# Rotary embedding of the retention heads in three pieces instead of one, with a second buffer

## The reference

```
h = rmsnorm(x, g_mix[l])
proj = h @ w_in[l]                      # split in q_r, k_r, v_r, g_r, q_s, k_s, v_s, gate_a, gate_b
q_r = rotary(q_r by 4 heads of 128)     # t1, t2 = the two halves of a head
k_r = rotary(k_r by 4 heads of 128)     # [t1*cos - t2*sin, t1*sin + t2*cos]
ret = retention(q_r, k_r, v_r)          # scores = q_r k_r * decay, times v_r
sb  = stick_breaking(q_s, k_s, v_s)     # weights from exp(log_beta + reversed cumulated sum)
merged = sigmoid(gate_a) * (norm(ret) * silu(g_r)) @ p_ret + sigmoid(gate_b) * sb @ p_sb
x = x + merged @ w_out ; x = x + relu(rmsnorm(x) @ w_up)^2 @ w_down
```

## Time and profile before

| | |
|---|---|
| median of three runs | 1245.2 us (1245.06 to 1245.97) |
| the profiled execution, its time | 1246.07 us |
| its span, first to last instruction | 1244.3 us |
| granted TensorE clock, mean | 0.998 |
| PE busy | 1213.6 us, 98% of the span |
| PEld busy | 1062.6 us, 85% |
| DVE busy | 890.3 us, 72% |
| ACT busy | 631.0 us, 51% |
| POOL busy | 56.3 us, 5% |
| DMA queue of the weights | 219.04 MB, 54.6% of 16 engines |

### The profile page before, as it was taken

One profiled execution on the slowest core, in us unless ns is written; L12 is line 12 of the kernel. 1 busy time (PEld: TensorE's weight loads), 2 busy tenths in 40 slices (PEclk: granted clock), 3 DMA queues, 4 the chain that ended last, 5 costly groups with the idle time before them and its releaser, 6 DMA issues.

```text
span 1244.3 us, 17057 instructions
## 1 busy us (share of the span) xinstructions
PE 1213.6 (98%) x6810; PEld 1062.6 (85%) x6810; DVE 890.3 (72%) x1040; ACT 631.0 (51%) x823; POOL 56.3 (5%) x70
## 2 busy tenths in 40 slices
PE   5999999999999999999999999999989999999998
PEld 4888888888888887888888888888879998988886
DVE  5577798888666676777888777666677766766665
ACT  4454576635343344555677445434458457443442
POOL 1000120001000000000220001000010000100000
PEclk9999999999999999999999999999999999999999
DMA  6854545555655656655555555565646334655552
GB/s 233 272 158 147 169 147 159 179 192 171 201 186 186 202 169 216 193 146 163 164 150 164 200 172 194 178 200 189 200 167 195 102 102 136 202 181 192 202 181 107
DMA packets 163082, 219.85 MB, mean 177 GB/s; under 512 B 5712, under 2 KB 134224, under 8 KB 163024
## 3 DMA queue, kind: packets, MB, share of 16 engines
q1 hardware_dynamic: 163024, 219.04, 54.6%
HBM read 217.98 MB, written 1.05 MB: 176 GB/s over the span
## 4 chain that ended last, share of the span: by engine, by line
PE 70%; issue 18%; DVE 5%; ACT 4%; DMA 2%; POOL 1%; SPq 0%; POOLq 0%; DVEq 0%; ACTq 0%
PE ps L497 69%; DVE w_lo L1317 2%; ACT w_hi L888 1%; DMA raw<-in_w_in_dram 1%; DMA decay_c<-in_decay_dram 1%; PE ps L532 1%; POOL retqkv L1284 1%; ACT junk L902 0%; DMA gain<-in_g_mix_dram 0%; DVE xs L1363 0%; DVE retqkv L1494 0%; DVE hT L1323 0%; ACT hz L1086 0%; ACT htmp L1094 0%; DVE htok L1347 0%
## 5 line engine op out<-in xcount | busy, mean ns | idle before, releaser
L1317 DVE TENSOR_TENSOR w_lo<-raw,w_hi 128x1024 fp32r<-128x1024 f32 x402 | 486.3, 1253 | 93.3 <-ACT w_hi L888 93.2
L888 ACT ACTIVATE w_hi<-raw 128x1024 fp32r<-128x1024 f32 x402 | 402.3, 1052 | 187.0 <-DMA raw<-in_w_up_dram 120.6
L497 PE MATMUL ps<-hT,w_hi 128*128 128x512 f32 (+1 forms) x1952 | 426.3, 365 | 6.8 <-DVE gr L1329 3.5
L497 PEld LDWEIGHTS ps<-hT,w_hi 128*128 128x128 f32 x1952 | 339.7, 190 | 62.2 <-issue 4.7
L497 PE MATMUL ps<-w_hi,uT 128*128 128x512 f32 x768 | 244.0, 390 | 0.0
L497 PE MATMUL ps<-hT,w_lo 128*128 128x256 f32 x1696 | 239.8, 283 | 0.0
L497 PEld LDWEIGHTS ps<-hT,w_lo 128*128 128x128 f32 x1696 | 225.4, 192 | 7.0
L894 ACT ACTIVATE carry<-ps 128x512 f32<-128x512 f32 x114 | 67.9, 596 | 261.8 <-PE ps L497 261.7
L497 PEld LDWEIGHTS ps<-w_hi,uT 128*128 128x128 f32 x768 | 144.4, 188 | 29.7 <-DVE uT L1323 0.6
L497 PE MATMUL ps<-w_lo,uT 128*128 128x512 f32 x384 | 149.9, 390 | 0.0
L497 PE MATMUL ps<-w_hi,hT 128*128 128x512 f32 (+1 forms) x480 | 142.3, 374 | 5.9 <-DVE w_lo L1317 4.5
(11 more groups left out here) (194 smaller groups left out, 920.2 us busy)
## 6 DMA issues: line engine op xcount, KB each, us to landing
raw<-in_w_in_dram SPq DMA_DIRECT2D x77, 1024.0 KB, 5.7
raw<-in_w_up_dram SPq DMA_DIRECT2D x48, 1024.0 KB, 5.3
raw<-in_w_down_dram SPq DMA_DIRECT2D x48, 1024.0 KB, 4.9
raw<-in_w_out_dram SPq DMA_DIRECT2D x12, 1024.0 KB, 4.9
raw<-in_p_sb_dram SPq DMA_DIRECT2D x8, 1024.0 KB, 5.2
raw<-in_p_ret_dram SPq DMA_DIRECT2D x8, 1024.0 KB, 5.0
xs<-in_x_dram SPq DMA_DIRECT2D x2, 512.0 KB, 6.4
gain<-in_g_mix_dram SPq DMA_DIRECT2D x2, 512.0 KB, 6.9
```

What stands on the lines that cost most here:

```text
L497: return pe.matmul(o, lhsT, rhs, start=start, stop=stop)
L888: act.activation(w_hi[:, s, half], raw[:, s, half], ACT.Copy).then_inc(hi_ready, 1)
L1317: last = dve.tensor_tensor(w_lo[:, s, half], raw[:, s, half], w_hi[:, s, half].bitcast(F32), ALU.subtract)
```

## The change

`rotate` becomes three steps with places of their own in `stages`: `swap` (ACT's exchange of the halves and POOL's cosines), `sines` (DVE's product with the sines) and `rotate` (DVE's sum). For the queries they stand at k = 16, 17 and 18, for the keys at k = 18, 19 and 20. On ACT `swap` is moved out of the stage function and is done before the conversion of piece k + 3. The keys' exchange writes into `gates[:, 0, 0:4, :]`, which lies idle then, instead of `ry`, and ACT's waits for `rest_split` and `rope_done` are gone.

```diff
-            if k in (18, 19):
-                todo.append(("rotate", k - 18))
+            for i in range(2):
+                for name, at_piece in (("swap", 16), ("sines", 17), ("rotate", 18)):
+                    if k == at_piece + 2 * i:
+                        todo.append((name, i))
...
+        def swapped(i):
+
+            return gates[:, 0, 0:4, :] if i else ry[:, :, :, :].rearrange("p a e t -> p (a e) t")
...
-                    elif name == "rotate":
-
-                        act.wait_ge(pair_free, use_of("rk", 1, L).count(3))
-                        act.wait_ge(rest_split, Place(3, (L, SB_H // 2)).count(1))
-                        if i:
-                            act.wait_ge(rope_done, Place(0, (L, 2)).count(1))
-                        swapped = ry[:, :, :, :].rearrange("p a e t -> p (a e) t")
-                        act.activation(swapped[0:P // 2], retqkv[P // 2:P, :, i, :], ACT.Copy)
-                        act.activation(swapped[P // 2:P], retqkv[0:P // 2, :, i, :], ACT.Copy).then_inc(turned, 1)
...
+                    for name, j in stages(k):
+                        if name == "swap":
+
+                            act.wait_ge(pair_free, use_of(("rq", "rk")[j], 1, L).count(3))
+                            act.activation(swapped(j)[0:P // 2], retqkv[P // 2:P, :, j, :], ACT.Copy)
+                            act.activation(swapped(j)[P // 2:P], retqkv[0:P // 2, :, j, :], ACT.Copy).then_inc(turned, 1)
                     if k < MIX_PIECES - 1:
                         convert(piece + AHEAD)
...
-                        elif name == "rotate":
+                        elif name == "swap":
 
                             pool.wait_ge(turned, Place(i, (L, 2)).count(1))
...
-                    elif name == "rotate":
-                        part = Place(i, (L, 2))
+                    elif name == "sines":
+                        part, tmp = Place(i, (L, 2)), swapped(i)
                         dve.wait_ge(turned, part.count(1))
                         dve.wait_ge(consts_in, 32)
-                        v, tmp = retqkv[:, :, i, :], ry[:, :, :, :].rearrange("p a e t -> p (a e) t")
                         dve.tensor_tensor(tmp, tmp, rope_c[:, 1:2, :].to_broadcast([P, RET_H, T]), ALU.mult).then_inc(rope_sin, 1)
+                    elif name == "rotate":
+                        part, v = Place(i, (L, 2)), retqkv[:, :, i, :]
                         dve.wait_ge(rope_cos, part.count(1))
                         dve.wait_ge(rope_sin, part.count(1))
-                        dve.tensor_tensor(v, v, tmp, ALU.add).then_inc(rope_done, 1)
+                        dve.tensor_tensor(v, v, swapped(i), ALU.add).then_inc(rope_done, 1)
```

## The result

| | before | after |
|---|---|---|
| median, runs beside each other | 1245.59 us (1245.06 to 1246.09) | 1260.16 us (1258.05 to 1260.96) |
| ratio after to before, 95% interval | | 1.0102 [1.009, 1.0114] |
| span of the profiled execution | 1244.3 us | 1258.6 us |
| granted TensorE clock, mean | 0.998 | 0.992 |

The change makes the kernel slower, as forecast, but by 14.6 us where 10.0 were forecast, and 1260.2 lies above the range, which ended at 1257.5.

What follows compares the result with a forecast made beforehand. PE, busy 98%, was taken to bound the kernel. Per layer -2.1 + 2.1 + 1.3 + 2.3 + 1.4 = +5.0 us, +10.0 in two layers, on 1245.2 gives 1255.2 us; range 1247.5 to 1257.5.

Steps and rivals of the forecast that it cites:

- What bounds: PE, busy 98% of the span; its late waits for `gr` at pieces 21 and 22 offered 2.1 us a layer.
- part 1: DVE no longer stands still in iteration 18, so PE's stalls at pieces 21 and 22 go: -2.1 us a layer.
- Part 2: ACT's two copies ahead of piece 19's conversion delay DVE's chain to `rest_lo`, with 0.05 us slack: +2.1 us a layer.
- Part 3: POOL's two cosine products block DVE's half conversions in the chain to `rest_lo`: +1.3 and +2.3 us a layer.
- Rival (1): POOL's second product misses DVE's chain: stall 3.4 us, 1247.8 us, or 1250.6 with the clock's sequel; chance 0.16.
- rival (3): POOL's products cost nothing, only the copies do: 2.1 against 2.1, no change, 1245.2 us; chance 0.08.
- rival (4): DVE's chain catches up before `rest_lo`, so only the gain stays: 1241.0 us; chance 0.08.
- Part 4: After PE's stall at `rest_lo` the granted clock falls to its lower level: +1.4 us a layer, bounds 0 and about 2.5.
- Rival (2): The stall at `rest_lo` is whole but the clock stays up: 3.6 us a layer, 1252.4 us; chance 0.10.
- Behind piece 22 nothing changes: Weight loads after piece 22 move with PE, so no further cost or gain was counted there.
- the signs named ahead: Profile after: `rest_lo` some 11 us, no `gr`, halves of some 2.5 and 3.4 us, cosines near 127.7 and 137.3, clock 0.50.

Runs made afterwards that it cites:

- after again: The changed kernel run and profiled once more with no edit, beside the kernel before: 1258.39 us, ratio 1.0084.
- exchange behind: Changed kernel with ACT's exchange of the halves behind the conversion of piece k + 3 instead of in front: 1248.51 us, ratio 1.0003.
- POOL late, both: Changed kernel with both POOL cosine products also waiting for `rest_lo` of the last pair, ACT's copies left in front: 1249.43 us, ratio 1.0005.
- POOL late, keys: Changed kernel with only the keys' POOL cosine product also waiting for `rest_lo`: 1255.05 us, ratio 1.0047.

## Why the prediction was right in its mechanism and wrong in its size

**What bounds, and part 1 (the saving).** Right. 2.1 us a layer were forecast, 2.23 and 2.28 measured; nothing else became late there.

**Part 2 (the copies in front of the chain).** Right: 2.1 forecast, 2.18 measured when the copies stand there alone.

**Part 3 (POOL).** Right, both products: 1.3 forecast and 1.24 measured for the first (3.42 - 2.18), 2.3 and 2.14 for the second (5.56 - 3.42). The stall was 5.55 us, 5.7 forecast. The Trainium skill's rule ("SBUF — State Buffer", "Who interferes with whom"), that one engine blocks the other for the whole instruction, agrees: instructions of DVE with both inputs in SBUF took 3.38 and 2.44 us instead of 1.2, and 3.08 instead of 0.96. What the rows add is that POOL got its turn between two instructions of DVE, though DVE had the next one ready (140.73 against halves at 139.99 and 141.12). Rival (1) falls with the experiment on the keys' product, rival (3) with the step from a stall of 2.18 us without POOL's products to 5.55 us with them, and rival (4) with the stall itself.

**Part 4 (the clock) is the term that was mis-sized.** I had taken 1.4 us a layer, the one price in the trace before, with bounds 0 and 2.5. Measured in the two profiles of the changed kernel: 1.74, 2.96, 2.45 and 3.20 us, 2.6 on average and twice above the bound. Rival (2) falls too. The price was taken over together with the length of its low stretch, and the length is what differed. A window's clock tells where the stretch begins or ends: 0.59 means that 0.82 us of it were at 0.50. Before, the stretch of the third layer ran from 932.6 to 936.1:

```profile
932.00:933.00 1.00, 0.73 (x5) 0.73 (x6) 1.00 (x2) 1.00 (x2) 0.00 (x0) 0.82 0.00 0
...
936.00:937.00 1.00, 1.00 (x10) 1.00 (x10) 0.75 (x1) 0.00 (x0) 0.00 (x0) 0.97 0.55 180
```

In the changed kernel it was about twice as long or longer. In its second profile:

```profile
141.00:142.00 1.00, 0.00 (x0) 0.00 (x0) 1.00 (x3) 0.00 (x0) 0.00 (x0) 0.63 1.04 368
...
148.00:149.00 1.00, 1.00 (x6) 0.81 (x5) 0.00 (x1) 0.00 (x0) 0.00 (x0) 0.96 0.00 0
...
598.00:599.00 1.00, 0.00 (x0) 0.00 (x0) 1.00 (x1) 0.46 (x1) 1.00 (x1) 0.82 0.88 190
...
608.00:609.00 1.00, 1.00 (x4) 0.81 (x3) 0.00 (x0) 0.00 (x0) 0.00 (x0) 0.56 0.00 0
```

The two stretches of the first profile of the changed kernel are equally long, but PE stood still through 2.8 us of the first, and it cost less. What counts is the time from PE's return to the end of the stretch:

| place | clock at 0.50 (windows) | PE works again at | us at work at 0.50 | us lost |
|---|---|---|---|---|
| before, third layer | 932.6 to 936.1 | 932.27 | 3.4 | 1.4 |
| after, layer 1 | 143.2 to 150.0 | 146.02 | 4.0 | 1.74 |
| after, layer 2 | 604.0 to 610.8 | 604.27 | 6.5 | 2.96 |
| after again, layer 1 | 141.3 to 148.1 | 142.65 | 5.4 | 2.45 |
| after again, layer 2 | 598.6 to 608.9 | 601.79 | 7.1 | 3.20 |

Each us at work at the lower level lost 0.41 to 0.46 us. By the length of the stall in front of it:

| stall of PE | us lost to the clock behind it |
|---|---|
| 2.0 (exchange behind) | none, 1.50 |
| 2.2 (POOL late, both) | 1.50, 1.49 |
| 3.4 (POOL late, keys) | 3.03, 2.85 |
| 5.55 (changed kernel, two profiles) | 1.74, 2.96, 2.45, 3.20 |

With 2.6 instead of 1.4 my sum is 5.55 + 2.6 - 2.25 = 5.9 a layer, 11.8 in all. The ledger of the second profile has 12.36 at piece 22 of the second layer, of which 0.1 belongs between the layers.

**What else put the time outside the range** is the value that the sum was added to. The corrected term alone gives 1245.2 + 11.8 = 1257.0, at the edge of the range but inside it, and all eight times of the changed kernel lie above it (1257.69 to 1261.44). The 1245.2 was the median of three runs, and the range had no term for the scatter of executions: the kernel before goes from 1245.1 to 1252.0, with a median of 1248.25 in the 25 runs of the second comparison. "Behind piece 22 nothing changes" held in sum, within 0.3 us in both profiles. But nothing was allowed for ahead of the change either, and there the first profile carried 3.34 us. The second carried none, and yet its execution took 1258.33 us: it stands 12.28 us behind the first profile of the kernel before, whose 1246.07 us were themselves above the median of three. Of the 14.35 us between the first two profiles 11.3 are the change's (8.41 - 3.34 and 14.60 - 8.37), 3.3 came before it, and the rest is -0.3 in the third layer. How much of the 1.0102 in the first comparison is scatter of that kind is not settled; the second comparison gave 1.0084, or 10.1 us between the medians, and 11.8 us would be 1.0095, which both intervals hold. That the second difference of medians comes so near the forecast 10.0 us is no confirmation of the clock term, which all four stalls exceeded.

Of the signs named ahead, `rest_lo` with about 11 us in two waits (10.4 visible, 11.1 by the ledger), no `gr`, the two blocked halves (2.44 and 3.38 us) and the clock at 0.50 all came. POOL's products started at 131.14 and 140.73, which less the 3.34 us of late arrival is 127.8 and 137.4, where 127.7 and 137.3 were forecast.

## What to carry to other kernels

Before a step is moved to an earlier place in a hand-written order, look for the wait of the bounding engine (the one that is busy nearly all the time) that ends last there, and at the chain behind it: here it had 0.05 us to spare, and each thing put ahead of it was paid in full. Count also what the moved instruction releases on other engines, since here the released products cost 3.4 of 5.6 us, and ask for the least edit that removes the stall: one buffer did it. A range for a few microseconds in a thousand needs several runs of the kernel before, not the spread of three.

## What the runs showed of the hardware

A stall of PE was dearer than its length: a low clock of 1.5 us in cost followed stalls of 2.0 to 2.2 us in three of four cases, and 1.7 to 3.2 us followed each one of 3.4 or 5.55 us, while the gaps of 1.9 us at piece 22 of the kernel before had no such sequel. The low stretch was longer behind the longer stall: in the first layer it ran from 140.9 to 144.3 behind the stall of 2.2 us and from 140.3 to 147.1 behind that of 3.4 us. What sets its length no run here isolates. And DVE instructions that read PSUM ran beside POOL's product at their usual 1.22 and 1.28 us, while those with both inputs in SBUF waited for it.
